# A two-block network kernel: 24 transposes ahead of the first, four VectorE steps moved in the first block, and the norm between sublayers placed and shared differently

## What is computed

```python
# first block
xn = rms_norm(h, norm_in_g)
q, k, v, g_ret, x_lru, g_lru = split(xn @ w_in)          # 12 chunks of 512 columns
xc = causal_depthwise_conv(x_lru, conv_w, conv_b)
o_ret = group_norm_heads(retention(rotary(q), rotary(k), v))   # 8 heads: (q k^T * decay) v
y_ret = o_ret * silu(g_ret)
y_lru = rg_lru(xc, gates) * silu(g_lru)                  # gates, exp, sqrt, then a scan in time
h = h + concat(y_ret, y_lru) @ w_out;  x = rms_norm(h, norm_out_g)
# second block, for l in 0, 1 (x, and in layer 0 the context too)
h = rms_norm(x) * g_pre_mix * (1 + sc1) + sh1            # norm, then modulation by scale and shift
o = merge(branches(h @ w_in[l]), w_branch[l]) @ w_out[l]
x = x + ga1 * rms_norm(o, g_post_mix)
f = conv_ffn(rms_norm(x) * g_pre_ffn * (1 + sc2) + sh2, w_up[l], conv, w_down[l])
x = x + ga2 * rms_norm(f, g_post_ffn)
```

## Time and profile before

| | us |
|---|---|
| median of 3 runs | 1716.9 (1715.5 to 1717.23) |
| the profiled execution | 1715.31 |
| its span | 1713.4 |
| PE busy in the span | 1672.2 (98%) |
| DVE busy | 1256.7 (73%) |
| ACT busy | 832.5 (49%) |

### The profile page before, as it was taken

The page is one execution under the profiler, slowest core; times in us unless marked ns, Lnnn a source line. Parts: engine busy times, 40 slices in busy tenths (PEclk is TensorE's granted clock), DMA queues, the critical chain, the costliest instruction groups (busy, mean ns, idle before and its releaser), DMA issues.

```text
span 1713.4 us, 25211 instructions
## 1 busy us (share of the span) xinstructions
PE 1672.2 (98%) x9824; PEld 1429.5 (83%) x9824; DVE 1256.7 (73%) x2201; ACT 832.5 (49%) x1346; POOL 0.2 (0%) x4
## 2 busy tenths in 40 slices
PE   7999999999999999999999999999999999999998
PEld 7888888777787778889888888889778989979997
DVE  7899767774779798856877786347756786678774
ACT  6665545553324344344444442336453455466653
POOL 0000000000000000000000000000000000000000
PEclk9999999999999999999999999999999999999999
DMA  8646542231234344542545556224222344546553
GB/s 334 232 160 223 198 145 87 79 143 62 63 96 169 115 149 165 210 144 91 145 135 196 197 196 221 93 80 136 99 86 63 122 159 144 172 156 174 196 195 125
DMA packets 79078, 254.91 MB, mean 149 GB/s; under 512 B 14320, under 2 KB 18672, under 8 KB 78320
## 3 DMA queue, kind: packets, MB, share of 16 engines
q1 hardware_dynamic: 73488, 244.91, 42.7%
q10 hardware_dynamic: 5472, 8.39, 1.5%
HBM read 252.19 MB, written 1.07 MB: 148 GB/s over the span
## 4 chain that ended last, share of the span: by engine, by line
PE 79%; DVE 13%; ACT 4%; issue 3%; DMA 1%; ACTq 0%; DVEq 0%
PE bank L693 66%; DVE w_lo L1725 3%; PE bank L824 3%; PE bank L995 2%; PE bank L981 2%; PE bank L1073 2%; PE bank L972 2%; ACT w_hi L1180 1%; PE bank L786 1%; DVE mod_w L1780 1%; PE bank L1062 1%; DVE probT L1780 1%; DMA w_raw<-in_weights 1%; DVE att L2273 1%; DVE bank L2271 0%
## 5 line engine op out<-in xcount | busy, mean ns | idle before, releaser
L1725 DVE TENSOR_TENSOR w_lo<-w_raw,w_hi 128x1024 fp32r<-128x1024 f32 (+1 forms) x356 | 427.0, 1211 | 258.7 <-ACT w_hi L1180 257.1
L1180 ACT ACTIVATE w_hi<-w_raw 128x1024 fp32r<-128x1024 f32 (+1 forms) x356 | 370.0, 1048 | 343.8 <-PE bank L693 292.0
L693 PE MATMUL bank<-hT_hi,w_hi 128*128 128x512 f32 (+1 forms) x1280 | 446.0, 348 | 1.7 <-issue 0.6
L693 PE MATMUL bank<-hT_hi,w_lo 128*128 128x512 f32 (+1 forms) x1280 | 437.6, 342 | 0.0
L693 PE MATMUL bank<-hT_lo,w_hi 128*128 128x512 f32 (+1 forms) x1280 | 437.3, 342 | 0.0
L693 PEld LDWEIGHTS bank<-hT_hi,w_hi 128*128 128x128 f32 x1280 | 242.7, 190 | 30.2 <-issue 3.1
L693 PEld LDWEIGHTS bank<-hT_hi,w_lo 128*128 128x128 f32 x1280 | 242.6, 189 | 28.2
L693 PEld LDWEIGHTS bank<-hT_lo,w_hi 128*128 128x128 f32 x1280 | 242.8, 190 | 27.0 <-issue 1.0
L1780 DVE SCALAR_TENSOR_TENSOR mod_w<-mod_w,c_rows 128x1024 f32<-128x1024 f32 x96 | 117.0, 1219 | 7.0 <-DMA mod_w<-in_mod_weights 7.0
L693 PE MATMUL bank<-w_hi,hT_hi 128*128 128x512 f32 x272 | 114.6, 421 | 0.0
L693 PE MATMUL bank<-w_lo,hT_hi 128*128 128x512 f32 x272 | 106.6, 392 | 0.0
(11 more groups left out here) (370 smaller groups left out, 2787.5 us busy)
## 6 DMA issues: line engine op xcount, KB each, us to landing
w_raw<-in_weights SPq DMA_DIRECT2D x356, 512.0 KB, 4.0
mod_w<-in_mod_weights SPq DMA_DIRECT2D x96, 512.0 KB, 3.9
nbias<-in_window_bias ACTq DMA_DIRECT2D x32, 128.0 KB, 3.0
resid_c<-in_ctx ACTq DMA_DIRECT2D x2, 1024.0 KB, 5.4
gain_mix<-gain_rows SPq DMA_DIRECT2D x3, 512.0 KB, 5.9
gain_ffn<-gain_rows SPq DMA_DIRECT2D x3, 512.0 KB, 4.0
c_rows<-in_conditions SPq DMA_DIRECT2D x1, 1024.0 KB, 5.7
gatew<-in_gate_weights SPq DMA_DIRECT2D x1, 1024.0 KB, 11.5
```

The costliest lines, as they stand in the source:

```text
L693: mm = pe.matmul(held[key][:, oc], st, mv_, start=(opens and k == 0 and t == 0 and i == 0), stop=(closes and k == tiles - 1 and t == 2), s ...
L1180: a.activation(w_hi[:, p % RING, :, used], w_raw[:, p % RING, :].rearrange("p (k n) -> p k n", k=KP)[:, :, used], ACT.Copy).then_inc(hi_re ...
L1725: v.tensor_tensor(w_lo[:, p % RING, :, used], w_raw[:, p % RING, :].rearrange("p (k n) -> p k n", k=KP)[:, :, used], w_hi[:, p % RING, :, ...
```

## The change

1. **Start.** TensorE does `WARM` = 24 transposes of the identity matrix as soon as it is loaded, ahead of the 16 real ones. VectorE splits each of the first four weight pieces ahead of the `xT_lo` of its group, not behind it, and one later piece ahead of the last `conv_pair`.
2. **Retention.** `ret_decay(0)` goes ahead of four modulation products, `ret_decay(1)` and the variance of head 0 ahead of the recurrence's multiplication; the first three scans go behind `ret_gate(0)`.
3. **Modulation.** In every norm of the second block ScalarE modulates the first half of each pair (from PSUM, then waits for its own result and copies), VectorE the second.
4. **Norm of tiles 0 and 1** into layer 0's FFN and into layer 1's mixing: `norm_T` goes into the last tile's products, two pieces from their end. The `norm_T` of tiles 2 and 3 goes one piece later, and both helpers' orders on ScalarE and VectorE change to match.

```diff
--- before.py
+++ after.py
+WARM = 24
...
+                        if within and len(of) == 1 and of[0][0] == banks[-1][0] and p == n - 3:
+                            within()
...
             pe.wait_ge(ident_loaded, 16)
+            for _ in range(WARM):
+                pe.transpose(psum(("xT", 0))[:, 0:P], ident, ident)
             for g in range(KD // 2):
...
                     for p in range(n):
-                        if gi == 0 and p == n // 2 and not late:
+                        if gi == 0 and p == (n // 2 if l and which == "ffn" else n - 1) and not late:
                             norm_T(l, which, 1)
...
-                if last:
-                    norm_T(l, "mix", 0)
...
                     gemm_tok(("wo", l, c), q_tts, mg_hi, mg_lo, by_bank=c == 1,
+                             within=None if last or c == 0 else lambda: norm_T(0, "ffn", 0),
                              inputs=None if c else lambda p, l=l: merged_ready.at((l, KP * p + KP - 1)))
-                norm_T(l, "ffn", 0)
+                if last:
+                    norm_T(l, "ffn", 0)
...
                     gemm_tok(("down", l, c), q_tts, fT_hi, fT_lo, tiles=FB, by_bank=c == 1,
+                             within=None if last or c == 0 else lambda: norm_T(1, "mix", 0),
                              inputs=None if c else lambda p, l=l: fT_ready.at((l, p)))
...
             def norm_hi(l, which, gi, p):

                 act.wait_ge(*hT_tmp_ready.at((l, which, gi, p)))
+                o = 0 if which == "mix" else 3
+                key, of = ("nT", l, which, gi, p), groups(l, which)[gi]
+                s = 1 - of[0] // 2
+                a.activation(ntmp_pair(l, which, gi, p)[:, 0, :], psum(key)[:, 0:len(of) * P], ACT.Identity,
+                             scale=scol[:, 2 * p, s:s + 1], bias=modT[:, l, 8 * o + 2 * p, s:s + 1]).then_inc(*A.drain(key))
+                act.wait_ge(*A.last())
                 a.activation(normed_pair(hT_hi, l, which, gi, p), ntmp_pair(l, which, gi, p), ACT.Copy)\
                     .then_inc(*A.tell(hT_hi_ready, (l, which, gi, p)))
...
                         if final:
-                            after = piece("w_up", l, 0) if which == "mix" else piece("w_in_2", l + 1, 0)
                             split_hi(after + 2)
+                            if two:
+                                norm_hi(*nxt, 0, 1)
                         else:
...
-                            if final:
+                            if final and not two:
                                 norm_hi(*nxt, 0, 0)
                             act.wait_ge(*post_ms.at((l, which, t)))
                             a.activation(rs[:, 4 + t:5 + t], ss[:, 24 + t:25 + t], ACT.Sqrt, scale=1.0 / D, bias=eps[:])\
                                 .then_inc(*A.tell(post_root, (l, which, t)))
                             if final:
                                 split_hi(after + 3)
-                                norm_hi(*nxt, 0, 1)
+                                norm_hi(*nxt, 0, 2 if two else 1)
                             if nxt is not None:
                                 if g == len(tts) - 2:
-                                    split_hi((piece("w_up", l, 0) if which == "mix" else piece("w_in_2", l + 1, 0)) + 1)
+                                    split_hi(after + 1)
+                                    if two:
+                                        split_hi(after + 2)
+                                        norm_hi(*nxt, 0, 0)
                                 norm_root(*nxt, t, o)
                             if final:
+                                if not two:
+                                    split_hi(after + 4)
+                                    norm_hi(*nxt, 0, 2)
                                 split_hi(after + 4)
-                                for gi, p in ((0, 2), (0, 3), (1, 0), (1, 1), (1, 2), (1, 3)):
+                                for gi, p in ((0, 3), (1, 0), (1, 1), (1, 2), (1, 3)):
                                     norm_hi(*nxt, gi, p)
...
             for g in range(KD // 2):
-                split_lo(g)
+                split_lo(g + 1)
                 dve.wait_ge(*xT_hi_ready.at(g))
...
             for i in range(2, 4):
                 conv_pair(i)
-                split_lo(9 + i)
+                split_lo(10 + i)
...
@@ -1936,25 +1968,24 @@
             dve.wait_ge(*lru_e2.at(HEADS - 1))
             v.tensor_scalar(xc[:], xc[:], 1.0, -1.0, ALU.min, ALU.mult).then_inc(*W.tell(lru_clamped, 0))
             split_lo(24)
-            mod_ops(2)
-            split_lo(25)
+            dve.wait_ge(decay_loaded, 16)
+            ret_decay(0)
             mod_ops(2)
             split_lo(26)
-            dve.wait_ge(decay_loaded, 16)
-            ret_decay(0)
+            mod_ops(2)
+            ret_decay(1)
+            ret_var_of(0)
             dve.wait_ge(*lru_mult.at(0))
             v.tensor_tensor(lru_i[:], lru_i[:], xc[:], ALU.mult).then_inc(*W.next())
+            ret_normed(0)
             dve.wait_ge(*W.last())
-            ret_decay(1)
-            ret_norm(0)
-            for n in range(3):
-                lru_scan(n)
             for g in range(2):
                 ahead((("in", 5), g))
                 dve.wait_ge(*drained_at((("in", 5), g)))
             ret_gate(0)
             ret_decay(2)
-            lru_scan(3)
+            for n in range(4):
+                lru_scan(n)
             ret_norm(1)
             ret_gate(1)
             ret_lo(0)
@@ -2053,12 +2084,9 @@
                 dve.wait_ge(*filled_at(key))
                 s = 1 - of[0] // 2
                 tmp = ntmp_pair(l, which, gi, p)
-                for j in range(2):
-                    k = 2 * p + j
-                    v.tensor_scalar(tmp[:, j, :], psum(key)[:, j * len(of) * P:(j + 1) * len(of) * P], scol[:, k, s:s + 1],
-                                    modT[:, l, 8 * o + k, s:s + 1], ALU.mult, ALU.add)\
-                        .then_inc(*(W.drain(key) if j else W.next()))
-                W.mark(hT_tmp_ready, (l, which, gi, p))
+                k = 2 * p + 1
+                v.tensor_scalar(tmp[:, 1, :], psum(key)[:, len(of) * P:2 * len(of) * P], scol[:, k, s:s + 1],
+                                modT[:, l, 8 * o + k, s:s + 1], ALU.mult, ALU.add).then_inc(*W.tell(hT_tmp_ready, (l, which, gi, p)))

             def norm_lo(l, which, gi, p):

@@ -2126,17 +2154,27 @@
                     key = ((w, l, 1), g)
                     o = o_of(which, t)
                     final = nxt is not None and g == len(tts) - 1
+                    two = len(tts) == 4
+                    if nxt is not None:
+                        after = piece("w_up", l, 0) if which == "mix" else piece("w_in_2", l + 1, 0)
                     if final:
-                        after = piece("w_up", l, 0) if which == "mix" else piece("w_in_2", l + 1, 0)
                         split_lo(after + 2)
-                        norm_tmp(*nxt, 0, 0)
+                        if two:
+                            norm_lo(*nxt, 0, 1)
+                            norm_tmp(*nxt, 0, 2)
+                        else:
+                            norm_tmp(*nxt, 0, 0)
                     else:
                         ahead(key)
                     dve.wait_ge(*stat_ready.at((l, which, t)))
                     v.tensor_tensor(ss[:, 24 + t:25 + t], ss[:, 8 + 2 * t:9 + 2 * t], ss[:, 9 + 2 * t:10 + 2 * t], ALU.add)\
                         .then_inc(*W.tell(post_ms, (l, which, t)))
                     v.tensor_tensor(o[:, COLS:D], psum(key)[:], gains[:, t // 2, COLS:D], ALU.mult).then_inc(*W.drain(key))
-                    if final:
+                    if final and two:
+                        norm_diag(*nxt, tts[-2])
+                        split_lo(after + 3)
+                        norm_lo(*nxt, 0, 2)
+                    elif final:
                         norm_lo(*nxt, 0, 0)
                         norm_tmp(*nxt, 0, 1)
                     dve.wait_ge(*W.last())
@@ -2148,18 +2186,28 @@
                         dve.wait_ge(ctx_loaded, 32)
                     v.scalar_tensor_tensor(r, o, ss[:, 28 + t:29 + t], r, ALU.mult, ALU.add)\
                         .then_inc(*W.tell(resid_ready, (*(nxt or ("end",)), t)))
-                    if final:
+                    if final and two:
+                        norm_tmp(*nxt, 0, 3)
+                    elif final:
                         norm_lo(*nxt, 0, 1)
                         split_lo(after + 3)
                         norm_tmp(*nxt, 0, 2)
                     if nxt is not None:
                         if g == len(tts) - 2:
-                            split_lo((piece("w_up", l, 0) if which == "mix" else piece("w_in_2", l + 1, 0)) + 1)
-                        norm_diag(*nxt, t)
+                            if two:
+                                norm_tmp(*nxt, 0, 0)
+                            split_lo(after + 1)
+                            if two:
```

(11 more changed lines are left out.)

16 lines of the change are left out of this document (12 added, 4 removed).

## The result

The changed kernel takes 1719.93 us (median of 12 runs, 1719.03 to 1720.95), the kernel before 1716.58 (12 runs, 1715.08 to 1719.34). The ratio is 1.0019, with a 95% interval of 1.001 to 1.0027: 3.35 us between the medians, a step that is small but clear of noise. 1719.4 was forecast. The profiled execution took 1719.32 with a span of 1717.5, 4.1 more than the span of before.

A forecast was written before the change was run, and what follows sets the result against it. TensorE's work was taken as the bound (busy 1672.2 of 1713.4 us), with VectorE setting the pace in the retention. Terms +0.2 + 1.4 - 0.2 + 1.1 + 0 = +2.5 on 1716.9 gave 1719.4 us, range 1714.0 to 1722.5.

The forecast's parts named there:

- VectorE as the bound of the retention: Retention: VectorE sets the pace and idles 1.6 for an earlier split, so TensorE's saved 3.61 isn't kept; term +1.4 us.
- The start: First transposes and weight splits: later input chain against the removed wait of 1.48 near 46; term +0.2 us.
- I take a change of level near their end, 10.3 for the last: Start: most of the 24 transposes run slow, the last ends at 10.3, and xT_hi comes 1.4 us later.
- 1.39 of slack less 0.1 taken from VectorE's lateness: Start, piece of 60.71: VectorE 1.5 later makes TensorE late by 1.5 - 1.3 = +0.2 us.
- The rule that spoke against the edit: Start: the full clock does not engage for transposes, so all 40 run slow and the sum would be 1720.8.
- rival 2: Start: all 24 transposes and the 16 behind run at 417 ns; +1.6, 1720.8 us; chance with neighbours 0.35.
- Into layer 0's FFN: Norm of tiles 0 and 1 moved earlier: the wait of 0.19 at 788.23 goes; term -0.2 us.
- Into layer 1's mixing: Norm of tiles 0 and 1 moved earlier: diagonal at 1163.3, norm_T(1) at 1163.4; term +1.1 us.
- cover is lost: Into layer 1's mixing: only three pieces of about 1.5 us lie between tile 3's bank fill and norm_T(1).
- about 2.1 lie in a row: Into layer 1's mixing: of the steps inserted into the diagonal's chain, about 2.1 us add to its 5.04.
- one operation longer on ScalarE but started with two halves at once: 0: Shared modulation into layer 1's FFN: the longer chain costs nothing; term 0, from -0.5 to +0.2 us.
- Rival 1: Retention mainly: the removed waits are gained, -3.6 there; about 1712.1 us, faster; chance 0.18.

The follow-up runs named there:

- e2: Changed kernel with VectorE's order in the retention as before (decay product behind the four modulation products, three scans ahead of the first gate); 1719.02 us.
- e10: Changed kernel with the hT_lo of step 2, ahead of layer 1's mixing, moved behind the last tile's residual on VectorE; 1718.41 us.
- e1: Changed kernel without the 24 transposes of the identity; 1716.47 us.
- e9: Kernel before with only the 24 transposes of the identity added; 1718.43 us.
- e7: Changed kernel keeping only the order of the first splits and the early norm into layer 0's FFN, the rest taken back; 1714.37 us.
- e8: Same as e7, but with the changed retention order, its early decay product not asking for the weight splits ahead; 1713.87 us.
- e5: Changed kernel whose early decay product of head 0 doesn't ask for the weight splits ahead of it; 1718.78 us.
- e6: Changed kernel with 11 transposes of the identity in place of 24; 1718.18 us.
- e3: Changed kernel with the norm into layer 1's mixing placed as before, modulation still shared; 1718.39 us.

## Why the forecast came out, and where its steps failed

The four terms of the sum were near: +0.2, +1.4, -0.2 and +1.1 were written, 0.46, 1.17, -0.50 and 1.20 were found, 2.3 in all for 2.5. That the median came within 0.6 of 1719.4 is in part luck all the same. Two causes outside the sum (the shared modulation and the 0.7 near 1390) make 1.8 more in the profile, and the medians differ by only 3.35 since the profiled execution of the kernel before lies 1.3 under its median and that of the changed kernel 0.6 under.

**VectorE as the bound of the retention: right.** Its rows had a little more idle time than was read from them: beside the 0.27 at 100.45 the roots at 108.38 and 115.37 have 0.27 each, and the gate at 103.28 has 0.13; that changes nothing. The steps came as written: no wait at `ret_out(0)`, one of 3.67 at `ret_turn(0)` (about 4 was said), VectorE idle 1.68 (1.6), head 3's product at 127.93 (127.7). TensorE reached `ret_turn(0)` earlier than was said: at 99.98, where it was at 105.61 before, 5.6 sooner and not 3.6, since the kernel before runs slow behind its wait at 95.19 (last section). As VectorE is the bound, that gave nothing. The term was +1.4 and measured +1.17; e2 takes it back and its profile gets just that (its times, 0.4 better, can't show it).

**The start: mis-sized.** +0.2 was the term, 0.46 the measurement. The step that failed is "I take a change of level near their end, 10.3 for the last": all but the last few ran slow and the real ones began at 11.06, so `xT_hi` was 2.08 late and not 1.4, and the first product began at 13.60 and not 12.85. In e10's profile, with the same start, they began at 10.38: the guess fits one execution and not another. The next step, 1.39 of slack less 0.1 taken from VectorE's lateness, gives with 1.82 the 0.5 that was found. The rule that spoke against the edit did not hold. The trace has 24 transposes and no product ahead of 11.06, and those after them take 272 ns instead of 421. The Trainium skill (TensorE: Matmul & The Clock Gate, "Part 4: PE-mode transpose") has transposes not engage the full clock; here transposes alone did. The slow warm-up of rival 2 came true for the 24, not for the 16 behind them. What I had not seen is that this edit holds a gain of 1.7 beside a loss of 2.2 (e1, e9).

**Into layer 0's FFN: right in sign**, -0.5 for -0.2; e7 and e8 have the same -0.5. The wait of 0.19 of the earlier trace rows is gone; where the other 0.3 comes from wasn't looked into.

**Into layer 1's mixing: right in size, half right in cause.** The diagonal was expected 1.1 late; it starts the second group 1.20 late. Taking off the 1.54 that TensorE was late already, the group starts at 1163.5, and 1163.4 was written. But the step "cover is lost" alone doesn't make it: without one inserted `hT_lo` (e10) 0.08 remains. Of the terms in "about 2.1 lie in a row", that step with its wait for ScalarE was the decisive one.

**Modulation: wrong.** The step "one operation longer on ScalarE but started with two halves at once: 0" fails in its second half. The diff shows ScalarE waiting for `hT_tmp_ready` ahead of its own half. It cost 0.4 at the first block's end and 0.6 into layer 1's FFN, and it makes the inserted `hT_lo` of the mixing wait (0.39).

**Not in the sum: 0.7 near 1390**, told below; its cause is open.

**Rival 1** (the removed waits are gained) fell where it was meant, in the retention: the 3.61 came back as 3.67 at the next place that VectorE feeds. The wait of 1.48 near 46, where VectorE has 1.39 of slack, is gained as soon as the transposes are left out (1.7 in e1 and e7).

## What to carry to other kernels

A wait on the busiest engine belongs to whoever feeds it: before moving a step ahead, look whether the feeder has idle time in that stretch, and which splits, loads or waits the moved helper brings along. A step inserted into a serial chain costs its own duration plus its wait for the other engine, since everything behind it on its queue waits too; without that one step the placement cost 0.08 instead of 1.20. And an edit with two halves is worth taking apart: here the order of the splits gains 1.7, and the transposes beside it lose more.

## What the runs showed of the hardware

**Transposes raise the clock.** With nothing but transposes ahead of them, the 16 real ones took 272 ns in the changed kernel and 417 in the kernel before, where the first product behind them already took 0.36, as in full run.

**Slow level after a short wait, in some profiles only.** Near 240 TensorE waits about 2.2 for a diagonal and then does 32 products. In nine of the twelve profiles they take 3.81, in e2 5.44, in e7 5.42 and in e5 5.35, with waits of 2.13 to 2.18 ahead in all twelve. First e2's row of the timeline and its stretches there (columns as in the earlier trace rows, the granted clock ahead of the last two):

```profile
239.34 5.44 PE L791 MATMUL bank<-diag,resid_x 128*128 128x128 f32 x32 [2.17 <-DVE diag L2077]
```

```profile
240.00:242.00 2.00, 2.00 (x11) 2.00 (x11) 0.54 (x1) 0.15 (x1) 0.00 (x0) 0.50 0.00 0
242.00:244.00 2.00, 2.00 (x16) 2.00 (x15) 1.02 (x2) 1.48 (x3) 0.00 (x0) 0.77 0.00 0
```

Then the changed kernel's row, and its stretches behind the wait of 2.90 at 127.93:

```profile
240.67 3.81 PE L791 MATMUL bank<-diag,resid_x 128*128 128x128 f32 x32 [2.18 <-DVE diag L2076]
```

```profile
128.00:130.00 2.00, 2.00 (x10) 2.00 (x11) 2.00 (x6) 1.97 (x3) 0.00 (x0) 0.50 0.05 21
130.00:132.00 2.00, 2.00 (x11) 2.00 (x11) 2.00 (x3) 2.00 (x4) 0.00 (x0) 0.50 0.17 25
```

A clock of 0.50 is the level of 1.2 GHz. Near 240 it cost e2, e5 and e7 1.0 to 1.6 each; the other profiles had none of it there. Behind 127.93 VectorE is the bound, and by 166 the changed kernel's shift is the 1.65 that it was ahead of the slow stretch: it cost nothing. The kernel before has such a stretch as well, behind the wait of 3.61 at 95.19:

```profile
97.00:99.00 2.00, 2.00 (x12) 2.00 (x11) 1.97 (x4) 1.97 (x4) 0.00 (x0) 0.50 0.21 84
```

Each kernel has one profile, so whether the stretch near 240 comes by the kernel or by the execution isn't shown. It may be why e1's times lie in two groups (1716.0 to 1716.5 and 1717.8 to 1718.1), which wasn't tested.

**The granted clock didn't show the slow start.** For the 24 transposes at 421 ns it reads 1.00, as it did for the 16 of the earlier trace rows at 417; only the durations show the level:

```profile
6.04:11.20 5.16, 5.16 (x26) 5.16 (x27) 3.88 (x8) 2.29 (x4) 0.00 (x0) 1.00 1.00 405
```

**DMA issue on ScalarE's queue, open.** Ahead of layer 1's attention ScalarE issues four loads of `nbias` in a row. They took 1.90 before and 2.65 in the changed kernel:

```profile
1368.12 2.65 ACTq L1527 DMA_DIRECT2D nbias<-in_window_bias  x4
```

All seven kernels with 24 transposes show 2.65 to 3.43, all five with 11 or none 1.90. ScalarE's next split comes as much later, and TensorE loses 0.7 to 1.5 near 1390 in all seven and nothing in the others. Neither the start of the issue nor TensorE's shift explains it (e6 issues later than e3 and e10, which are slow). Why 24 transposes at the start should matter there isn't known.
